# Triangular inverses of a gated delta rule: 32x32 diagonal blocks on tiles of the array instead of whole 128x128 matrices

## The chip, the core and the metric

One core of a Trainium2 chip runs the whole program. The metric is the device time of one execution in microseconds (us), taken as the median of several runs. A difference of about 0.3% is what a measurement of this kernel can tell from no change.

The core's engines are PE (TensorE, with its weight loads shown apart as PEld), DVE (VectorE), ACT (ScalarE), POOL (GpSimd) and SP (which here issues DMAs). They run side by side and wait for each other on semaphores.

## What is computed

Two layers of a decoder trunk on 512 tokens of width 1024. Each layer has four token mixers, a merge of their outputs through gates, and a gated feed-forward part. The change is inside one of the mixers, the gated delta rule (4 heads, chunks of 64 tokens), of which this is the part that matters:

```python
decay = where(tril, exp(G[..., :, None] - G[..., None, :]), 0)
L = where(strict, einsum('bnhid,bnhjd->bnhij', k * beta, k) * decay, 0)
T = triangular_solve(eye + L, eye, lower=True, unit_diagonal=True)   # the inverse
u = einsum('bnhij,bnhjd->bnhid', T, v * beta)
w = einsum('bnhij,bnhjd->bnhid', T, k * beta * exp(G))
# then a recurrence over the chunks with u, w and a state
```

The kernel takes chunks of 128 tokens, so there are 4 chunks x 4 heads = 16 lower triangular matrices of 128x128 a layer, and each is inverted.

## The kernel before

**Weights.** All weights stream from memory in slabs of 512 KB: SP loads a slab to `raw` (2 buffers), ACT rounds it to a high part `wH` (L1061), POOL or DVE makes the low part `wL` (L2034, L1422), and PE multiplies with three products for each pair of tiles (L489 to L491). 3 slabs can be split ahead.

**Fillers.** A layer's projections that nobody needs at once are kept as fillers. `fill(n)` on PE does n of them (`column_tile`, 24 matmuls of 128x512 each), and the table `FILL` says how many stand at which place of the mixers. The same `fill` on ACT moves the result out of its bank (L1064), splits the next slab (L1061) and stores the result. The order on every engine is that in which the code is written; each engine works through its own list.

**The inverse.** The 16 matrices (units) stand transposed or not in four buffers of the tile `arena`: `mL` holds L, `mU` the inverse as it grows (transposed, upper triangular), `mT` the transpose of `mU`, `mY` a product. They are handled in four batches of 4 units, one PSUM bank a batch. The method doubles the size of the blocks whose inverse is known: 1, 2, 4, ... 64 to 128, seven levels.

- Level 0: PE transposes L (L697), DVE masks it to pairs (L1717) and subtracts it from the identity (L1719).
- Levels 1 to 6, for each of the four batches: PE forms `mL`·`mU` (`y_product`, L708) and transposes `mU` (`t_transpose`, L718); DVE masks the product (L1723) to the blocks of this level (`lev`); ACT copies the transpose out (L1233); PE multiplies the two (`u_product`, L728); DVE subtracts the result from `mU` (L1729). Every product is of full 128x128 matrices whatever the level, since the mask picks the blocks.
- The batches are staggered by hand so that PE has another batch to work on while DVE and ACT serve one.

A float32 matmul is recorded as two instructions on PE and two weight loads (two passes); a transpose as one. So `L708 x8` is four products.

**Around it.** Ahead of the inverse PE forms k·k and q·k (L688), then does two fillers (`FILL["skq"]`), while POOL makes `qd` (L2081) and DVE multiplies q·k by the decay (L1705, `at_part`). One filler stands after the fifth of the six levels (`FILL["level"]`). After the inverse PE forms w (L753), and the recurrence over the four chunks begins (L762 and on).

Of the kernel before, what the change touches and what calls it, by code (L numbers as in the profile page):

```python
# [23 lines left out]
P = 128  # L24
# [45 lines left out]
        "turn": 0, "skq": 2, "level": [0, 0, 0, 0, 1, 0], "chunk": [1, 1, 1, 0], "oss": 1,  # L70
# [19 lines left out]
def _slabs():  # L90
# [8 lines left out]
    for dt in range(KT):  # L99
# [12 lines left out]
             "du_ps": 24, "fg_tanh": 22, "ga_ready": 44, "gate_tanh": 8, "gdn_done": 2, "gexp_ready": 1,  # L112
# [11 lines left out]
             "ss_ps": 2, "st_ready": 17, "su_ps": 4, "t_cos": 3, "t_ps": 24, "t_ready": 24, "t_sin": 4,  # L124
             "tanh_ready": 6, "tr_ps": 4, "tr_taken": 4, "trig_done": 6, "u0_ready": 8, "u_chunks": 4,
             "u_ready": 24, "vn_ps": 4, "vn_ready": 4, "vt_ps": 1, "vt_ready": 1, "wexp_ready": 16, "wt_ps": 4,
             "wt_ready": 4, "x_ready": 2, "xo_ready": 8, "y0_ps": 4, "y5_ps": 2, "y5_ready": 2, "y5_sq": 2,
             "y5_tanh": 4, "y_ps": 24, "y_ready": 24, "z_copied": 16, "z_tanh": 2}
# [21 lines left out]
def _const_columns():  # L150
    at = 0
    for name, n in [("ones", P), ("ident", P), ("blk", P), ("le", P), ("ge", P), ("lt", P),
                    ("gt", P), ("lev", 7 * P), ("rot", P), ("freq", 1), ("stack", 32), ("cneg", NT * NCMP),
                    ("c01", NT * NCMP), ("t", P)]:
        CK[name] = (at, n)
        at += n
    return at
# [34 lines left out]
def program(nc, a_x, a_pos, a_const, a_pack, a_w, a_gates, a_out):  # L192
    with ExitStack() as ctx:
# [64 lines left out]
        lev = cst("lev").rearrange("p (l c) -> p l c", l=7)  # L258
# [20 lines left out]
            skk_ps l_part skq_ps at_part y0_ps u0_ready  # L279
            y_ps y_ready du_ps u_ready t_ps t_ready wt_ps wt_ready  # L280
# [37 lines left out]
        mL, mU, mT, mY = mats  # L318
        cv = arena[:, 8192:11264].rearrange("p (t s) -> p t s", t=6)
# [108 lines left out]
        with nc.Block() as block:  # L428
# [30 lines left out]
            def _(pe):  # L459
                for layer in range(DEPTH):  # L460
# [230 lines left out]
                    fill(FILL["skq"])  # L691

                    pe.wait_ge(*of("bt_taken", 6))
                    for b in range(4):
                        pe.wait_ge(*of("at_part", b + 1))
                        for j in range(4):
                            last = nc.tensor.transpose(PS[2 + b][:, P * j:P * j + P], mL[:, 4 * b + j, :], ident)  # L697
                        last.then_inc(q["y0_ps"], 1)
                    def y_product(n):
                        b = n % 4  # L700
                        if n >= 4:
                            pe.wait_ge(*of("u_ready", n - 3))
                        else:
                            pe.wait_ge(*of("u0_ready", 2 * n + 2))
                        if n >= 2:
                            pe.wait_ge(*of("y_ready", n - 1))
                        for j in range(4):
                            last = mm(PS[2 + n % 2][:, P * j:P * j + P], mL[:, 4 * b + j, :], mU[:, 4 * b + j, :],  # L708
                                      start=True, stop=True)
                        last.then_inc(q["y_ps"], 1)  # L710

                    def t_transpose(n):

                        b = n % 4
                        if n >= 2:
                            pe.wait_ge(*of("t_ready", n - 1))
                        for j in range(4):
                            last = nc.tensor.transpose(PS[6 + n % 2][:, P * j:P * j + P], mU[:, 4 * b + j, :], ident)  # L718
                        last.then_inc(q["t_ps"], 1)

                    def u_product(n):
                        b = n % 4
                        pe.wait_ge(*of("y_ready", n + 1))
                        pe.wait_ge(*of("t_ready", n + 1))
                        if n >= 2:
                            pe.wait_ge(*of("u_ready", n - 1))
                        for j in range(4):
                            last = mm(PS[4 + n % 2][:, P * j:P * j + P], mT[:, 4 * b + j, :], mY[:, 4 * b + j, :],  # L728
                                      start=True, stop=True)
                        last.then_inc(q["du_ps"], 1)  # L730

                    pe.wait_ge(*of("kc_ready", 1))
                    for lv in range(6):
                        n = 4 * lv
                        y_product(n)
                        t_transpose(n)
                        y_product(n + 1)
                        t_transpose(n + 1)
                        u_product(n)
                        y_product(n + 2)  # L740
                        t_transpose(n + 2)
                        u_product(n + 1)
                        y_product(n + 3)
                        t_transpose(n + 3)
                        u_product(n + 2)
                        u_product(n + 3)
                        fill(FILL["level"][lv])

                    pe.wait_ge(*of("u_ready", 24))
# [277 lines left out]
            def _(a):  # L1027
                act = nc.scalar.activation
                chain, split = [0], [0]
                for layer in range(DEPTH):  # L1030
# [200 lines left out]
                    for n in range(24):  # L1231
                        a.wait_ge(*of("t_ps", n + 1))
                        act(mT_flat[:, S * (n % 4):S * (n % 4) + S], PS[6 + n % 2][:, :], ACT.Copy).then_inc(q["t_ready"], 1)  # L1233
                        if n % 4 == 3:
                            fill(FILL["level"][n // 4])
# [166 lines left out]
            def _(v):  # L1402
                chain = [0]
                for layer in range(DEPTH):
# [295 lines left out]

                    v.wait_ge(*of("skq_ps", 4))
                    v.wait_ge(*of("qd_ready", 8))
# [5 lines left out]
                    def four(x):  # L1708
                        return x.unsqueeze(1).broadcast_to([P, 4, P])

                    def bank4(b):
                        return PS[b][:, :].rearrange("p (u c) -> p u c", u=4)

                    for b in range(4):
                        u = slice(4 * b, 4 * b + 4)
                        v.wait_ge(*of("y0_ps", b + 1))
                        tt_(mY[:, u, :], bank4(2 + b), four(lev[:, 0, :]), M).then_inc(q["u0_ready"], 1)  # L1717
                        v.wait_ge(*of("u0_ready", 2 * b + 1))
                        tt_(mU[:, u, :], four(ident), mY[:, u, :], SU).then_inc(q["u0_ready"], 1)  # L1719
                    def y_mask(n):  # L1720
                        b = n % 4
                        v.wait_ge(*of("y_ps", n + 1))
                        tt_(mY[:, 4 * b:4 * b + 4, :], bank4(2 + n % 2), four(lev[:, 1 + n // 4, :]), M)\  # L1723
                            .then_inc(q["y_ready"], 1)

                    def u_update(n):
                        u = slice(4 * (n % 4), 4 * (n % 4) + 4)
# [540 lines left out]
```

## Time and profile before

| | us |
|---|---|
| median of 3 runs | 2095.03 (2090.07 to 2096.05) |
| the profiled execution | 2093.96 |
| its span, first to last instruction | 2092.1 |
| PE busy | 2003.3 |
| DVE busy | 1120.0 |
| ACT busy | 779.3 |
| POOL busy | 421.1 |
| last product of q·k to the first product for w, layer 1 | 191.49 to 268.32 |

The profiled execution is 1.9 us longer than its span and 1.1 us under the median. Times in the trace are counted from the start of the span. Matmuls overlap, so PE's busy time is a union of intervals.

### The profile page before, as it was taken

To read this page: it belongs to the slowest core of one execution; us is meant where nothing else is said; L and a number is where in the kernel's file an instruction comes from. 1 tells how busy PE (TensorE), PEld (TensorE's weight loads), DVE (VectorE), ACT (ScalarE), POOL (GpSimd) and SP (SyncE) were. 2 spreads that over 40 slices of the span, in tenths; PEclk is the share of its full clock that TensorE was granted. 3 is DMA by queue.
4 is the path that set the end of the run, shared out by engine and by line. 5 is a ranking of instruction groups with operands and counts; after the bars stand their busy time and mean duration, and the time that the engine had idled before them with its cause. 6 is when DMAs were issued, how large, how long until landed. Compare 5 with 4: busy or idle time off the path is not lost.

```text
span 2092.1 us, 25542 instructions
## 1 busy us (share of the span) xinstructions
PE 2003.3 (96%) x9988; PEld 1607.9 (77%) x9988; DVE 1120.0 (54%) x1702; ACT 779.3 (37%) x1182; POOL 421.1 (20%) x240
## 2 busy tenths in 40 slices
PE   7999989899999999999999999999999999999999
PEld 5677978567677888888876789776677778888887
DVE  6955547553466555543369265565523765555422
ACT  5542253553344332222244422526532543232221
POOL 2436012223153000000035350122321610000000
PEclk9999999999999999999999989999999999999999
DMA  5332012212153333333343210112121633333332
GB/s 199 115 117 62 11 56 81 76 51 76 56 216 107 101 100 96 96 101 101 111 161 96 89 53 16 61 66 81 58 74 59 228 101 91 93 98 101 101 101 101
DMA packets 57133, 196.45 MB, mean 94 GB/s; under 512 B 6464, under 2 KB 6976, under 8 KB 54848
## 3 DMA queue, kind: packets, MB, share of 16 engines
q1 hardware_dynamic: 42912, 152.49, 23.2%
q10 hardware_dynamic: 14112, 42.41, 5.3%
q8 instruction: 79, 1.29, 0.3%
q14 instruction: 30, 0.25, 0.0%
HBM read 176.01 MB, written 18.87 MB: 93 GB/s over the span
## 4 chain that ended last, share of the span: by engine, by line
PE 86%; DVE 9%; ACT 2%; POOL 1%; issue 1%; DMA 1%; SPq 0%; ACTq 0%; DVEq 0%; PEldq 0%; POOLq 0%
PE bank L489 22%; PE bank L491 22%; PE bank L490 22%; PE bank L728 2%; PE bank L708 2%; PE bank L958 2%; PE bank L846 2%; PE bank L919 1%; PE bank L827 1%; PE bank L718 1%; DVE arena L1804 1%; PE bank L855 1%; PE bank L627 1%; DVE arena L1465 1%; PE bank L836 1%
## 5 line engine op out<-in xcount | busy, mean ns | idle before, releaser
L489 PE MATMUL bank<-hH,wH 128*128 128x512 f32 (+1 forms) x1536 | 616.7, 402 | 22.2 <-DVE hL L1431 10.2
L490 PE MATMUL bank<-hL,wH 128*128 128x512 f32 (+1 forms) x1536 | 604.3, 393 | 0.0
L491 PE MATMUL bank<-hH,wL 128*128 128x512 f32 (+1 forms) x1536 | 604.2, 393 | 0.0
L2034 POOL TENSOR_TENSOR wL<-raw,wH 128x1024 fp32r<-128x1024 f32 (+1 forms) x114 | 274.5, 2411 | 1188.0 <-ACT wH L1061 1187.8
L1061 ACT ACTIVATE wH<-raw 128x1024 fp32r<-128x1024 f32 (+1 forms) x276 | 288.1, 1046 | 255.9 <-PE bank L491 215.6
L489 PEld LDWEIGHTS bank<-hH,wH 128*128 128x128 f32 (+1 forms) x1536 | 291.0, 189 | 99.9 <-issue 25.1
L491 PEld LDWEIGHTS bank<-hH,wL 128*128 128x128 f32 (+1 forms) x1536 | 290.4, 189 | 64.7 <-issue 0.8
L490 PEld LDWEIGHTS bank<-hL,wH 128*128 128x128 f32 (+1 forms) x1536 | 291.0, 189 | 61.9 <-issue 2.6
L1422 DVE TENSOR_TENSOR wL<-raw,wH 128x1024 fp32r<-128x1024 f32 x162 | 214.1, 1321 | 212.5 <-ACT wH L1061 211.8
L1064 ACT ACTIVATE gst<-bank 128x512 f32<-128x512 f32 x64 | 38.2, 597 | 275.4 <-PE bank L491 275.4
L491 PE MATMUL bank<-hidH,wL 128*128 128x512 f32 x352 | 140.4, 399 | 0.0
L490 PE MATMUL bank<-hidL,wH 128*128 128x512 f32 x352 | 138.7, 394 | 0.0
L489 PE MATMUL bank<-hidH,wH 128*128 128x512 f32 x352 | 138.0, 392 | 0.0
L1384 ACT ACTIVATE hidH<-arena 128x512 fp32r<-128x512 f32 x44 | 27.9, 633 | 191.3 <-DVE arena L2002 191.3
L1920 DVE TENSOR_REDUCE small<-bank 128x1 f32<-128x128 f32 (+3 forms) x64 | 30.8, 489 | 114.4 <-PE bank L921 113.0
L2104 POOL TENSOR_TENSOR arena<-arena 128x512 f32<-128x512 f32 x48 | 79.2, 1651 | 25.4 <-DVE arena L1962 21.4
L490 PEld LDWEIGHTS bank<-hidL,wH 128*128 128x128 f32 x352 | 66.1, 188 | 17.0
L489 PEld LDWEIGHTS bank<-hidH,wH 128*128 128x128 f32 x352 | 66.1, 188 | 15.9
L491 PEld LDWEIGHTS bank<-hidH,wL 128*128 128x128 f32 x352 | 66.1, 188 | 15.3
L1381 ACT ACTIVATE comp<-comp 128x512 f32<-128x512 f32 x44 | 27.8, 632 | 127.6 <-DVE comp L1993 127.6
L1233 ACT ACTIVATE arena<-bank 128x512 f32<-128x512 f32 x48 | 28.6, 597 | 78.8 <-PE bank L718 78.8
L1993 DVE TENSOR_TENSOR comp<-bank,vt 128x512 f32<-128x512 f32 x44 | 30.4, 691 | 48.4 <-PE bank L491 43.0
(398 smaller groups left out, 2835.6 us busy)
## 6 DMA issues: line engine op xcount, KB each, us to landing
raw<-weights SPq DMA_DIRECT2D x279, 512.0 KB, 3.5
gates<-gst ACTq DMA_DIRECT2D x64, 256.0 KB, 2.4
gload<-gates ACTq DMA_DIRECT2D x16, 1024.0 KB, 7.2
arena<-weights ACTq DMA_DIRECT2D x10, 512.0 KB, 5.4
xT<-x SPq DMA_DIRECT2D x4, 512.0 KB, 6.3
pj<-weights ACTq DMA_DIRECT2D x4, 512.0 KB, 4.0
out<-xT SPq DMA_DIRECT2D x8, 256.0 KB, 4.2
const<-constants SPq DMA_DIRECT2D x1, 1100.5 KB, 6.6
```

The costliest lines, as they stand in the source:

```text
L489: mm(out, a[0], b[0], start=start, stop=False)
L490: mm(out, a[0], b[1], start=False, stop=False)
L491: return mm(out, a[1], b[0], start=False, stop=stop)
L708: last = mm(PS[2 + n % 2][:, P * j:P * j + P], mL[:, 4 * b + j, :], mU[:, 4 * b + j, :], start=True, stop=True)
L728: last = mm(PS[4 + n % 2][:, P * j:P * j + P], mT[:, 4 * b + j, :], mY[:, 4 * b + j, :], start=True, stop=True)
L846: last = mm(out[:, P * (j - kb):S - P * kb], cst("ge") if j == kb else ones, sb_sp(h, j)[:, P * j:S], start=(j == kb), stop=(j == NT - 1), ...
L958: last = mm(PS[6 + br][:, HD * h:HD * h + HD], npt[:, kb, P * h:P * h + P], nvt[:, kb, HD * br:HD * br + HD], start=(kb == 0), stop=(kb == ...
L1061: act(h, x, ACT.Copy).then_inc(q["w_high"], 1)
L1064: act(out, stream(name)[:, :], ACT.Copy, scale=scale).then_inc(q["proj_taken"], 1)
L1422: tt_(wL[:, ORD[i] % SPLIT], raw[:, i % RING], wH[:, ORD[i] % SPLIT].bitcast(F32), SU)\
L2034: tt_(l, x, h.bitcast(F32), SU).then_inc(slab_taken[i % RING], 1)
L2104: ins = tt_(mtmp[:, dt % 2, 0, :], mtmp[:, dt % 2, 0, :], mtmp[:, dt % 2, m, :], A_)
```

## The change

The inverse is built in two parts.

- **Diagonal blocks of 32.** Each 128x128 matrix has four diagonal blocks of 32x32. Blocks, not whole matrices, go through levels 0 to 4 (block sizes 1 to 32). A matmul takes rows 32b to 32b+32 of its operands and writes the same rows of a bank: one 32x32 tile of the array for each b. Both the inverse (`uc32`) and its transpose (`ut32`) are carried, each updated by its own product, so there is no transpose. The 16 units are in two halves of 8, which share nothing; PE's two products for a level are `block_y` (32 matmuls a half) and `block_u` (64 a half, 32 at level 0).
- **Levels 32 and 64 as blocks.** The blocks are copied into `mU` (zeroed by POOL ahead of time) and `ut64`. Then the off-diagonal blocks of 32 (80 matmuls of 32x32) and of 64 (32 matmuls of 64x64) are formed with products of just those blocks; copies go half to ACT, half to DVE.
- **Order.** `block_y` of level 0 stands ahead of the two fillers; DVE's first masks stand ahead of its multiplications by the decay (L1705). The filler inside the inverse stays after the fifth level (n = 4), which is now the last of the small ones. ACT's 24 copies (L1233) are gone; ACT has 6 copies after level 4, ahead of its part of that filler, and 5 in the block levels.
- The table of masks shrinks from 7x128 to 5x32 columns, with an identity of 32 columns.

The core of the diff:

```diff
+                    def block_y(n, g):
+                        out = PS[(2, 7)[g]]
+                        for u in UNIT_HALF[g]:
+                            for b in range(4):
+                                last = mm(out[rows(b), 32 * (u % 8):32 * (u % 8) + 32], mL[rows(b), u, rows(b)],
+                                          uc32[rows(b), u, :] if n else cst("id32")[rows(b), :], start=True, stop=True)
+                        last.then_inc(q["y_ps"], 1)
+                    def block_u(n, g):
+                        for u in UNIT_HALF[g]:
+                            c = slice(32 * (u % 8), 32 * (u % 8) + 32)
+                            if n:
+                                for b in range(4):
+                                    mm(PS[3 + g][rows(b), c], ut32[rows(b), u, :], y32[rows(b), u, :], start=True, stop=True)
+                            for b in range(4):
+                                last = mm(PS[5 + g][rows(b), c], y32[rows(b), u, :],
+                                          ut32[rows(b), u, :] if n else cst("id32")[rows(b), :], start=True, stop=True)
+                        last.then_inc(q["du_ps"], 1)
+                    pe.wait_ge(*of("bt_taken", 6))
+                    for g in range(2):
+                        block_y(0, g)
                     fill(FILL["skq"])
-                    for lv in range(6):
-                        y_product(n) ... t_transpose(n) ... u_product(n)
+                    pe.wait_ge(*of("at_part", 4))
+                    for n in range(5):
+                        for g in range(2):
+                            if n:
+                                pe.wait_ge(*of("u_ready", 2 * n + g - 1))
+                                block_y(n, g)
+                        for g in range(2):
+                            pe.wait_ge(*of("y_ready", 2 * n + g + 1))
+                            block_u(n, g)
+                        fill(FILL["level"][n])
+                    pe.wait_ge(*of("u_ready", 10))
...
+                    for g in range(2):
+                        for u in UNIT_HALF[g]:
+                            last = mm(PS[5 + g][0:64, HD * (u % 8):HD * (u % 8) + HD], mL[64:128, u, 0:64], mU[64:128, u, 64:128],
+                                      start=True, stop=True)
+                        last.then_inc(q["y_ps"], 1)
...
+                    for g in range(2):
+                        pe.wait_ge(*of(("y_copied", "y_ready")[g], (2, 12)[g]))
+                        for u in UNIT_HALF[g]:
+                            last = mm(PS[(7, 2)[g]][0:64, HD * (u % 8):HD * (u % 8) + HD], ut64[:, u, :], y64[:, u, :],
+                                      start=True, stop=True)
+                        last.then_inc(q["du_ps"], 1)
```

On PE, before, one level for two of its four batches stands like this (first level; L708 products with `mU`, L718 transposes, L728 the second product):

```order
L708 MATMUL bank<-arena 128x128 [waits u0_ready,kc_ready]
L708 MATMUL bank<-arena 128x128 x3
L718 MATMUL bank<-const,arena 128x128 x4
L708 MATMUL bank<-arena 128x128 [waits u0_ready]
L708 MATMUL bank<-arena 128x128 x3
L718 MATMUL bank<-const,arena 128x128 x4
L728 MATMUL bank<-arena 128x128 [waits t_ready,y_ready]
L728 MATMUL bank<-arena 128x128 x3
```

On PE in the changed kernel, the same place, from the start of level 1 (L703 is `block_y`, L712 and L714 the two products of `block_u`):

```order
L703 MATMUL bank<-arena 32x32 [waits u_ready]
L703 MATMUL bank<-arena 32x32 x31
L703 MATMUL bank<-arena 32x32 [waits u_ready]
L703 MATMUL bank<-arena 32x32 x31
L712 MATMUL bank<-arena 32x32 [waits y_ready]
L712 MATMUL bank<-arena 32x32 x3
L714 MATMUL bank<-arena 32x32 x4
L712 MATMUL bank<-arena 32x32 x4
```

A level was 48 instructions of 128x128 (16 + 16 transposes + 16) and is now 192 of 32x32 (64 + 64 + 64), with four waits instead of one for each batch and step.

On DVE, between the multiplication of k·k by the decay and level 1, before:

```order
L1699 TENSOR_TENSOR arena<-bank,arena 128x512 [waits dmask_ready,skk_ps] x4
L1705 TENSOR_TENSOR arena<-bank,arena 128x512 [waits qd_ready,skq_ps]
L1705 TENSOR_TENSOR arena<-bank,arena 128x512 x3
L1717 TENSOR_TENSOR arena<-bank,const 128x512 [waits y0_ps]
L1719 TENSOR_TENSOR arena<-const,arena 128x512 [waits u0_ready]
```

and after (L1734 and L1759 are the old L1699 and L1705; L1749 masks, L1771 and L1772 update the inverse and its transpose, L1774 starts the transpose):

```order
L1734 TENSOR_TENSOR arena<-bank,arena 128x512 [waits dmask_ready,skk_ps] x4
L1749 TENSOR_TENSOR arena<-bank,const 128x256 [waits y_ps,qd_ready]
L1749 TENSOR_TENSOR arena<-bank,const 128x256 [waits y_ps]
L1755 TENSOR_TENSOR arena<-const,arena 128x256 [waits y_ready] x2
L1759 TENSOR_TENSOR arena<-bank,arena 128x512 [waits skq_ps]
L1759 TENSOR_TENSOR arena<-bank,arena 128x512 x3
L1763 MEMSET arena 32x16x32 [waits at_part]
L1774 TENSOR_TENSOR arena<-const,bank 128x256 [waits du_ps] x2
L1749 TENSOR_TENSOR arena<-bank,const 128x256 [waits y_ps] x2
L1771 TENSOR_TENSOR arena<-arena,bank 128x256 [waits du_ps]
L1772 TENSOR_TENSOR arena<-arena,bank 128x256
```

Four instructions of 128x256 came ahead of the multiplications by the decay, and a level is 6 instructions of 128x256 instead of 8 of 128x512.

On PE, from the end of the filler inside the inverse to w, the changed kernel has (L737, L744 and L745 the blocks of 32, L751 and L758 those of 64, L767 is w); before, the sixth full level and then w stood here:

```order
L737 MATMUL bank<-arena 32x32 [waits u_ready]
L737 MATMUL bank<-arena 32x32 x31
L744 MATMUL bank<-arena 32x32 [waits y_ready,y_copied]
...
L751 MATMUL bank<-arena 64x64 [waits u_ready,u_copied]
L751 MATMUL bank<-arena 64x64 x15
L758 MATMUL bank<-arena 64x64 [waits y_copied,u_copied]
L758 MATMUL bank<-arena 64x64 x7
L758 MATMUL bank<-arena 64x64 [waits y_ready]
L758 MATMUL bank<-arena 64x64 x7
L767 MATMUL bank<-arena,pj 64x128 [waits u_ready,u_copied]
```

The last level became a chain of five steps, each of which waits for copies by ACT and DVE.

## Rows read from the trace of the kernel before

**Rows 1.** The page's part 1 (busy time) and part 4 (share of the last chain).

```profile
PE 2003.3 (96%) x9988; PEld 1607.9 (77%) x9988; DVE 1120.0 (54%) x1702; ACT 779.3 (37%) x1182; POOL 421.1 (20%) x240
...
PE 86%; DVE 9%; ACT 2%; POOL 1%; issue 1%; DMA 1%; SPq 0%; ACTq 0%; DVEq 0%; PEldq 0%; POOLq 0%
```

**Rows 2.** The chain, 170 to 320: start us, us, engine, tile, line.

```profile
190.40 1.16 PE bank L688 x8
...
226.17 0.89 PE bank L708 x8
227.06 0.44 PE bank L718 x4
...
235.14 0.89 PE bank L708 x8
...
268.32 1.99 PE bank L753 x32
```

**Rows 3.** Windows: busy us of each engine (instructions), granted clock, DMA share.

```profile
191.49:202.30 10.81, 10.81 (x49) 8.95 (x49) 2.48 (x4) 1.54 (x2) 8.61 (x10) 1.00 0.25 76
202.30:268.30 66.00, 62.19 (x522) 60.23 (x520) 39.64 (x57) 17.31 (x28) 4.74 (x2) 1.00 0.11 33
252.80:258.40 5.60, 5.60 (x27) 4.63 (x26) 0.72 (x2) 0.00 (x0) 0.00 (x0) 1.00 0.00 0
...
1239.00:1305.00 66.00, 62.17 (x523) 60.27 (x523) 39.75 (x57) 17.31 (x28) 4.74 (x2) 1.00 0.11 33
```

**Rows 4.** Windows of L600 (69.30), then of L627 (161.30): PE, PEld, clock.

```profile
69.30:69.35 0.05, 0.03 (x4) 0.03 (x5) 1.00 0.00 0
...
161.30:161.37 0.07, 0.03 (x4) 0.03 (x5) 1.00 0.00 0
```

**Rows 5.** Sequencer of PE, waits in three windows: ns min/median/max, first to last start.

```profile
L706 PEldq EVENT_SEMAPHORE  x2: 51/51/51, 216.1 to 216.4; - x2
...
L726 PEldq EVENT_SEMAPHORE  x1: 1480/1480/1480, 217.7 to 217.7; - x1
...
L706 PEldq EVENT_SEMAPHORE  x1: 51/51/51, 219.3 to 219.3; - x1
```

**Rows 6.** Timeline: start, us, engine, line, shapes; idle before it and its releaser.

```profile
161.34 7.16 PE L627 MATMUL bank<-vt,pj 128*32 128x128 f32 x128
...
198.49 2.48 DVE L1705 TENSOR_TENSOR arena<-bank,arena 128x512 f32<-128x512 f32 x4 [8.14 <-POOL arena L2081]
...
199.01 2.40 POOL L2034 TENSOR_TENSOR wL<-raw,wH 128x1024 fp32r<-128x1024 f32 x1 [0.62 <-ACT wH L1061]
...
227.53 0.60 ACT L1233 ACTIVATE arena<-bank 128x512 f32<-128x512 f32 x1 [2.60 <-PE bank L718]
228.43 0.69 DVE L1723 TENSOR_TENSOR arena<-bank,const 128x512 f32<-128x512 f32 x1 [0.64 <-PE bank L708]
...
258.67 0.60 ACT L1064 ACTIVATE gst<-bank 128x512 f32<-128x512 f32 x1 [6.82 <-PE bank L491]
259.16 1.05 ACT L1061 ACTIVATE wH<-raw 128x1024 fp32r<-128x1024 f32 x1
...
270.77 1.10 PE L762 MATMUL bank<-pj,arena 128*128 128x64 f32 x8 [0.48 <-ACT arena L1238]
```

**Rows 7.** Groups by line and shape, window 268 to 303 and the first layer.

```profile
L1745 DVE COPY arena<-bank 128x256 f32<-128x256 f32 x4 | 1.7, 425 | 12.6 <-PE bank L770 12.6
...
L627 PE MATMUL bank<-vt,pj 128*32 128x32 f32 x32 | 4.4, 229 | 0.0
```

**Rows 8.** Windows of PE alone: busy us (instructions), granted clock.

```profile
466.20:469.48 3.28, 3.28 (x33) 1.00 0.00 0
469.48:473.00 3.52, 3.52 (x10) 0.52 0.00 0
473.00:476.00 3.00, 3.00 (x15) 0.99 0.00 0
...
1217.20:1230.80 13.60, 13.60 (x66) 0.50 0.12 39
```

More of the change, by code:

```diff
@@ L69 @@
 FILL = {"blocks": [1, 1, 1, 1, 1, 1, 1, 1], "hidden": 1, "gelu": 1, "gsum": 2, "qk": 1, "grow": 1,
[L70 removed]
+        "turn": 0, "skq": 2, "level": [0, 0, 0, 0, 1], "chunk": [1, 1, 1, 0], "oss": 1,
         "s5": [3, 2], "glu": 2, "sb": [2, 1, 1, 1, 1], "norms": 1, "rot": 2,
@@ L690, in _ @@
                             last.then_inc(q[done], 1)
-                    fill(FILL["skq"])
[L693 to L708, printed above, removed]
+                    UNIT_HALF = [range(0, 8), range(8, 16)]
@@ new lines, in _ @@
+                    pe.wait_ge(*of("u_ready", 10))
+                    for u in range(16):
+                        for b in (0, 2):
+                            last = mm(PS[2][rows(b), 32 * u:32 * u + 32], mL[rows(b + 1), u, rows(b)], uc32[rows(b + 1), u, :],
+                                      start=True, stop=True)
+                    last.then_inc(q["y_ps"], 1)
+                    pe.wait_ge(*of("y_copied", 1))
+                    pe.wait_ge(*of("y_ready", 11))
+                    for u in range(16):
+                        for b in (0, 2):
+                            mm(PS[3][rows(b), 32 * u:32 * u + 32], ut32[rows(b), u, :], y32[rows(b), u, :], start=True, stop=True)
+                        last = mm(PS[4][rows(1), 32 * u:32 * u + 32], y32[rows(0), u, :], ut32[rows(0), u, :], start=True, stop=True)
@@ L721, in u_product @@
[L721 to L728, printed above, removed]
+                    pe.wait_ge(*of("u_copied", 2))
@@ new lines, in _ @@
+                    for n in range(5):
+                        if n:
+                            for g in range(2):
+                                y_mask(n, g)
+                        for g in range(2):
+                            v.wait_ge(*of("du_ps", 2 * n + g + 1))
+                            if n:
+                                tt_(half_of(uc32, g), half_of(uc32, g), half_bank(3 + g), SU)
+                                tt_(half_of(ut32, g), half_of(ut32, g), half_bank(5 + g), SU).then_inc(q["u_ready"], 1)
+                            else:
+                                tt_(half_of(ut32, g), eight(cst("id32")), half_bank(5 + g), SU).then_inc(q["u_ready"], 1)
@@ L2222, in _constants @@
     put("gt", r > c)
-    lev = np.zeros((P, 7, P))
-    for n in range(7):
+    lev = np.zeros((P, 5, 32))
+    a, b = r % 32, np.arange(32)[None, :]
+    for n in range(5):
         s = 1 << n
-        lev[:, n] = (r // (2 * s) == c // (2 * s)) & (r % (2 * s) < s) & (c % (2 * s) >= s)
+        lev[:, n] = (a // (2 * s) == b // (2 * s)) & (a % (2 * s) < s) & (b % (2 * s) >= s)
     put("lev", lev)
+    put("id32", a == b)
     rot = np.zeros((P, P))
```

141 lines of the change are left out of this document (74 added, 67 removed).

## The prediction

> **What bounds the kernel now.** I read the busy shares first, then the last chain, then that chain inside the inverse, then the windows around it. PE is busy 96% of the span and the chain runs through PE for 86% [rows 1], so PE's own time counts nearly everywhere. In the inverse, one level of six takes 235.14 - 226.17 = 8.97 us [rows 2]. Its 80 PE instructions (16 products of two passes, 16 transposes of one, 16 products of two) go at 0.89 us for 8, which is 0.111 each or 8.9 us a level: PE is full. DVE's and ACT's pieces are done inside that time [rows 6]. The windows say the same for both layers: PE is busy 62.2 of 66.0 us from 202.3 and from 1239, DVE 39.6, ACT 17.3, at full clock [rows 3]. So the stage is worth what PE issues in it. I count it from the end of the last q·k products (191.49) to the first product for w (268.32): 76.8 us a layer [rows 2], 10.8 for two fillers and 5.6 for the third [rows 3], and 60.4 for the inverse.
>
> **What the change takes off.** All 60.4 us of that: the transposes of level 0, six full levels, and the waits at both ends. ACT loses 24 copies, DVE 56 operations of 128x512; neither was late, so this alone is worth nothing.
>
> **What it puts there.** Per layer 976 matmuls of 32x32 (64 and 64 at level 0, 4 x 192, 32 and 48 at level 32) and 32 of 64x64. Before there were 304 of 128x128. What one of the 32x32 costs decides everything; the trace has none, so I bound it.
>
> - *From below: the tiles.* The products of 32-column weights write four column tiles in turn, and four of them start within 0.07 us (0.05 for L600) [rows 4]: tiles side by side run together. A pass over 128 columns takes 0.111 us, so one over 32 columns takes about 0.028 (estimate), a product of two passes 0.056, and four at once 14 ns each.
> - *The feed.* PE's sequencer must hand out each product. Two of its waits, with eight matmuls between them, stand 0.3 us apart, 0.05 of it the wait itself: about 31 ns each. After a wait that ends at 217.7 + 1.48 = 219.2, four products are out by 219.3: about 25 ns each [rows 5].
> - *From above.* If tiles took turns, 56 ns. 128 passes of L627 take 7.16 us [rows 6], 112 ns a product, but those have up to 128 columns.
>
> I take 25 ns, the feed, since it lies above the 14 ns of the tiles and a level will keep the feed going without a pause; 14 and 56 stay as ends. A product of 64x64 on one tile: two passes over 64 columns, 2 x 0.055 = 0.11 us; the upper end is 0.22, from the 8 passes over 64 columns in 1.10 us of L762, whose weights are twice as wide [rows 6].
>
> The Trainium skill, TensorE: Matmul & The Clock Gate (Part 1), states that start-to-start never drops below about 25 ns however small N is. Taken for each pass, that would be 50 ns a product, and the case of a slow feed below. Here the trace disagrees at least for a handful of passes: four starts in 0.05 us [rows 4].
>
> **The other engines in a level.** DVE has six operations of 128x256; the nearest row, a copy of that size from PSUM, takes 0.425 us [rows 7], back to back about 0.35 (a 128x512 repeats every 0.62: 2.48 for four [rows 6]). From the last matmul's start to the next engine I allow 0.27 (a 32-column pass is recorded with 0.229 [rows 7]), and 0.06 back. The two halves alternate: while DVE masks one half (0.27 + 0.42 + 0.06 = 0.75) PE does the other's 32 products (0.8 us at 25 ns), so PE does not wait there. After `block_u` DVE needs 0.27 + 0.35 + 0.42 + 0.06 = 1.1 us for a half, PE is busy 0.8 with the other half's `block_y`: 0.3 us of wait a level, three times. A level is then 192 x 0.025 + 0.3 = 5.1 us. If the products took 14 ns, the loop of DVE and PE would set a level at 3.3.
>
> **The block levels.** After the filler ACT must first empty its bank and split a slab (0.60 + 1.05 [rows 6]), so its copy of the first product ends about 2.5 us after the filler where PE needed 0.8: 1.8 us of wait. Then a DVE copy ahead of the products of 64 (0.27 + 0.6 + 0.06 = 0.9; 0.60 is ACT's copy of 128x512 and these hold as many columns [rows 6]), nothing between the two products of 64 since their halves cover each other, and 0.9 before w: 3.7 with the small pieces.
>
> **Moved and added steps, costed at nothing.** `block_y` of level 0 is now ahead of the fillers; its time is counted, and it delays them by 1.6 us. DVE's four new operations (1.7 us) delay the decay multiplications, which ran from 198.49 to 200.97 [rows 6]: they end about 202.7, and PE, with two fillers and 1.6 us, comes at 203.9. That is 1.2 us of cover; without it, PE waits. POOL's clearing of 128x2048 stands ahead of its next low part, which began at 199.01; a 128x1024 operation takes 2.4 us, so at most 4.8 us [rows 6], and the next filler is 20 us away. ACT waits for the clearing, long done. SP's queue changes nowhere but in 360 KB less of constants at the start, early enough to be worth zero.
>
> **The sum at full clock.** 976 x 0.025 = 24.4, 32 x 0.11 = 3.5, fillers 10.8 + 5.5 = 16.3, waits 0.9 + 3.7 = 4.6: 48.8 us in place of 76.8, a gain of 28.0 a layer.
>
> **The clock.** After 3.3 us of PE with products of 31 columns (L889, 33 instructions) the granted clock was 0.52 for the next 3.5 us, with PE busy all the time: 10 filler matmuls there, against 15 in the next 3.0 [rows 8]. In layer 2 it was 0.50 for 13.6 us from 1217.2 on, after a stretch of short bursts. These are the levels of 1.2 and 2.4 GHz. The new stage is 25 us of products of 32 columns, the nearest thing in the trace is L889, so I take the lower level through it. It costs 32 x 0.104 = 3.3 us at the products of 64, 1.7 at the filler (half of 3.4), 1.9 at w (1.99 us [rows 2] at twice the time), and 1.2 in the levels (the tiles now need 28 ns, 3 over the feed, for about half of the 768). Together 8.1; the gain is 19.9 a layer, 39.8 in all.
>
> 2093.96 - 39.8 = 2054.2 for the profiled execution; the median of the runs lies 1.1 above that: **2055 us**.
>
> **Rivals.**
>
> 1. *The clock holds.* All four tiles busy may look like a busy array, as it does through L627 (clock 1.00 in its window [rows 4]). Gain 28.0 a layer: 2039. For it: PE never pauses. Against: L889, also without a pause.
> 2. *The tiles set the pace.* The feed is faster than I read it (rows with one decimal) and a level is the loop of 3.3 to 4.0 us, at 14 to 18 ns: gain 33.6 to 36.7 a layer, 2022 to 2028.
> 3. *The feed is slower.* 976 products are 4000 instructions in 25 us; nothing in the trace asks for such a rate for longer than a few. At 31 to 40 ns (first reading of rows 5, and half as much again) each ns costs 0.98 us a layer and the 0.9 us of waits in the levels go: with the lower clock's 6.9 the gain is 16.1 at 31 and 7.4 at 40, 2063 to 2080; at 50 ns it would be 2100.
> 4. *The tiles take turns* (slower). The four tiles of a product group write the same bank at the same columns from different rows of the array. L600 and L627 use all 128 rows, so no row shows this. If a bank takes one row group at a time, a product costs its own 56 ns: a level is 192 x 0.056 = 10.75 us where it was 8.97 and the stage 77.3 at full clock: 2096. At the lower clock the 56 become 112, and the stage is 62 us longer than now: 2219. If each also waits for the last one's write, 0.229 [rows 7], the kernel is over 2400. It decides from about 48 ns a product (22.0 us of gain left without the 0.9 of waits, over 0.976 us for each ns).
>
> The Trainium skill, TensorEngine Tiling (Array Packing), Gotcha 1, states that different row tiles cannot access the same PSUM bank simultaneously. By that rule it would be rival 4. No run here shows it; the case for the forecast is only that different partitions of the bank are written.
>
> **How the numbers follow.** Forecast 2055: 0.34. Clock holds: 0.25. Tiles set the pace: 0.11. Slower feed: 0.16, nearly all faster than now. Turns: 0.12. Something else that eats the gain, near no change: 0.02. A measurement of this kernel can tell 0.3%, that is 6 us, from no change. Faster by more than that: 0.34 + 0.25 + 0.11 + 0.14 = 0.84. Within: 0.04. Slower: 0.12. The range takes in the forecast, both quick cases and the slower feed up to 40 ns, and leaves out the turns and the ends: 2022 to 2088.
>
> **What the profile would show.** A level of `block_y` and `block_u`: 5 us if the feed sets it, 3.3 if the loop does, 10.75 if tiles take turns, with starts of the four tiles 7 ns or 28 ns and more apart. The granted clock from 210 on: 0.5 (forecast) or 1.0. DVE idle before L1771 for PE, and PE not idle before L712. After the filler, PE idle until ACT's copy L1262. The stage 48.8 us (clock holds) or about 55, with w 1.9 longer. I am wrong if a level takes over 8 us, if the decay multiplications (L1759) end after PE has come, or if the next stages give the time back: the chunks and the S5 part wait for DVE and ACT, which have more slack now, not less.

## The result, and the profile after

The changed kernel takes **2103.75 us** (median of six runs, 2098.14 to 2109.39), the kernel before, run beside it, 2094.87 (2090.07 to 2096.05): a ratio of 1.0045, with a 95% interval from 1.0031 to 1.0059. It is slower by about 9 us or 0.45%, where the forecast was 2055 and the range 2022 to 2088. The profiled executions span 2104.3 and 2092.1 us.

The page of the changed kernel, parts 1, 3 and 4 (they answer to [rows 1]; the first line is busy us, share and instructions of each engine):

```profile
PE 1972.1 (94%) x13028; PEld 1572.7 (75%) x13028; DVE 1065.5 (51%) x1660; ACT 763.9 (36%) x1156; POOL 426.1 (20%) x242
...
q8 instruction: 103, 1.69, 0.3%
...
PE 82%; DVE 10%; issue 4%; ACT 2%; POOL 2%; DMA 1%; POOLq 0%; SPq 0%; ACTq 0%; DVEq 0%; PEldq 0%
```

PE is busy for 31 us less than before, as meant. But "issue", time in which the engine waits for nothing that the profile shows, went from 1% to 4% of the chain, and PE has 3040 matmuls and 3040 weight loads more. That is 6080 instructions more, and the queue that carries the instructions moved 103 packets of 16 KB where the kernel before moved 79:

```profile
q8 instruction: 79, 1.29, 0.3%
```

24 packets for 6080 instructions fits 256 instructions of 64 bytes in each. Where the issue time lies is told by the chain through levels 1 and 2 and the start of level 3 of the first layer (start us, us, what; the longest pieces), which stands where [rows 2] had one product after the other:

```profile
204.14 1.04 PE bank L703 x85
205.18 2.46 issue
207.64 0.41 PE bank L703 x26
208.95 3.51 issue
212.46 0.26 PE bank L712 x2
214.40 2.07 issue
216.46 0.26 PE bank L712 x2
217.10 1.60 PE bank L703 x98
218.70 1.49 issue
220.19 0.58 PE bank L703 x26
222.12 1.80 issue
223.92 0.26 PE bank L712 x2
225.85 1.53 issue
227.38 0.26 PE bank L712 x2
228.01 1.60 PE bank L703 x98
229.62 1.21 issue
```

Two things are to be seen. In a burst the products are quicker than forecast. The chain holds only 85 of the 100 passes of the first burst of level 1, so the rate is read from the timeline; the granted clock there is 1.00:

```profile
204.10 1.08 PE L703 MATMUL bank<-arena 32*32 32x32 f32 x100
```

Without the last pass's own 0.19 us, 100 passes start within 0.89 us: 9 ns each, 18 a product. At a clock of 0.50 it is 13 a pass and 26 a product, from the first `block_y` of the second layer (1.86 us less 0.24):

```profile
1230.93 1.86 PE bank L703 x128
```

And no burst lasts: PE works 1.3 to 2.3 us and stands still for 1.2 to 3.5, three times a level. PE's waits over the whole span put a sum to this (us in total, times, longest):

```profile
PE bank L712 <- issue: 30.5, 16, 3.5
PE bank L703 <- issue: 13.9, 8, 2.5
```

These are 24 stalls, three in each of four levels of both layers, and 44.4 us or 22.2 a layer. The groups by line from the end of one stall to the end of the next, 230.8 to 234.2 (columns as in part 5 of a page: line, engine, operation, tiles, count, busy us, mean ns, idle time before), count what is in a burst:

```profile
L712 PE MATMUL bank<-arena 32*32 32x32 f32 x52 | 1.6, 236 | 0.0
L712 PEld LDWEIGHTS bank<-arena 32*32 32x32 f32 x52 | 1.5, 152 | 0.0
L714 PE MATMUL bank<-arena 32*32 32x32 f32 x48 | 1.5, 236 | 0.0
L714 PEld LDWEIGHTS bank<-arena 32*32 32x32 f32 x48 | 1.4, 152 | 0.0
L703 PE MATMUL bank<-arena 32*32 32x32 f32 x28 | 0.6, 239 | 1.2 <-issue 1.2
L703 PEld LDWEIGHTS bank<-arena 32*32 32x32 f32 x28 | 0.5, 148 | 1.3 <-issue 1.3
```

128 matmuls and 128 loads: 256 instructions, one packet, whatever lines they come from. The other bursts between two stalls of levels 1 to 3 hold 128 and 128 as well. The DMA view of the changed kernel over the same levels, 217 to 249 us, in slices of 0.8 us (GB/s), shows the packets one by one:

```profile
GB/s 0 20 0 0 0 20 0 0 0 20 0 0 0 0 20 0 0 0 20 0 0 0 0 20 0 0 0 20 0 0 0 20 0 0 0 20 0 0 0 0
...
q8 instruction: 9, 0.15, 1.8%
```

Nine packets, four to five slices apart: 27.2 us for eight steps, 3.4 each, and three fetches are a level. In the same window the kernel before needs three:

```profile
q8 instruction: 3, 0.05, 0.8%
```

The levels themselves, in windows from the first `block_y` (L703) of levels 2, 3 and 4 to that of the next, or to the filler (window, length, then busy us and instructions of each engine, granted clock, DMA share):

```profile
217.10:228.01 10.91, 6.09 (x403) 5.56 (x396) 2.35 (x6) 0.00 (x0) 0.00 (x0) 0.50 0.02 5
228.01:238.38 10.37, 6.11 (x403) 5.58 (x396) 2.35 (x6) 0.00 (x0) 0.00 (x0) 0.50 0.02 5
238.38:249.01 10.63, 6.09 (x383) 5.49 (x373) 2.35 (x6) 0.00 (x0) 0.00 (x0) 0.50 0.02 5
```

A level takes 10.4 to 10.9 us, where one took 8.97 before and 5.1 was forecast. Level 1, whose fetches run beside the slabs of weights, takes 12.96 (204.14 to 217.10). From the end of the q·k products (190.55) to w (268.66) are 78.1 us, against 76.8. Most of the rest of the loss lies behind: the chunk stage from w to the output's L795 (now L809), before and after,

```profile
268.32:305.34 37.02, 32.25 (x217) 28.12 (x217) 19.38 (x31) 19.12 (x32) 7.08 (x3) 1.00 0.18 56
```

```profile
268.66:309.13 40.47, 35.76 (x217) 31.68 (x217) 19.30 (x30) 19.09 (x32) 7.09 (x3) 0.88 0.16 52
```

has the same instructions and takes 3.4 us longer, at a granted clock of 0.88 in place of 1.00. Half of this, 1.7 us, is w itself at its start.

### The profile page after: what moved, and what is told of

Read it like the earlier page. It is cut to its first block, busy times and chain, and to the rows that moved or that the text cites. A ratio compares the mean times of both kernels' runs of the same rounds, so it can differ in the third digit from the quotient of the medians.

```text
span 2104.3 us, 31472 instructions
## 1 busy us (share of the span) xinstructions
PE 1972.1 (94%) x13028; PEld 1572.7 (75%) x13028; DVE 1065.5 (51%) x1660; ACT 763.9 (36%) x1156; POOL 426.1 (20%) x242
## 4 chain that ended last, share of the span: by engine, by line
PE 82%; DVE 10%; issue 4%; ACT 2%; POOL 2%; DMA 1%; POOLq 0%; SPq 0%; ACTq 0%; DVEq 0%; PEldq 0%
PE bank L491 21%; PE bank L493 21%; PE bank L492 21%; PE bank L860 2%; PE bank L972 2%; PE bank L933 1%; DVE wL L1457 1%; DVE arena L2010 1%; DVE arena L1852 1%; PE bank L703 1%; PE bank L869 1%; PE bank L841 1%; PE bank L712 1%; PE bank L714 1%; PE bank L629 1%
## 5 line engine op out<-in xcount | busy, mean ns | idle before, releaser
L1457 DVE TENSOR_TENSOR wL<-raw,wH 128x1024 fp32r<-128x1024 f32 x162 | 214.1, 1322 | 212.9 <-ACT wH L1075 212.2
L492 PEld LDWEIGHTS bank<-hidL,wH 128*128 128x128 f32 x352 | 66.1, 188 | 17.1
L712 PE MATMUL bank<-arena 32*32 32x32 f32 x1024 | 31.8, 234 | 30.5 <-issue 30.5
```

Source lines behind the costliest of these rows:

```text
L492: mm(out, a[0], b[1], start=False, stop=False)
L712: mm(PS[3 + g][rows(b), c], ut32[rows(b), u, :], y32[rows(b), u, :], start=True, stop=True)
L1457: tt_(wL[:, ORD[i] % SPLIT], raw[:, i % RING], wH[:, ORD[i] % SPLIT].bitcast(F32), SU)\
```

## The experiments

**Theory A, the instruction fetch.** PE can hold one block of 256 instructions beyond the one that it works on, and a block arrives about 3.5 us after the last one was begun. A product of 32x32 in float32 is four instructions (two passes, each a load and a matmul), so 64 products are a block, and no matter how fast the array is, they cost 3.5 us: 55 ns a product. The rivals: the array is slow (tiles take turns, or the lower clock), or the loop between TensorE and VectorE sets the level.

**wide: twice the columns, the same instructions.** Every product of levels 1 to 4 streams 64 columns.

```
-  uc32[rows(b), u, :]
+  uc32[rows(b), u - u % 2:u - u % 2 + 2, :]      # and likewise y32, ut32; 64 columns of out
```

> Each 32x32 product of levels 1 to 4 streams 64 columns instead of 32 (its own and its neighbour's), so the values are not the reference's; the instructions, waits and tiles stay the same in number. Theory A (the instruction fetch: the engine gets its instructions in blocks of 16 KB, and one block, 64 products, arrives every 3.5 us): a level, read from the first L703 of one level to that of the next, stays at 10.4 to 10.9 us and the whole kernel within 5 us of 2104. Theory B (the array: tiles take turns, or the lower clock makes a pass slow): a product costs by its columns, and a level goes from 10.4 to 15 us or more, the kernel to 2140 or more.

2099.80 us in one run. The windows of levels 2 to 4:

```profile
218.04:228.52 10.48, 7.58 (x398) 7.01 (x392) 2.35 (x6) 0.00 (x0) 0.00 (x0) 0.83 0.02 5
228.52:238.89 10.37, 6.22 (x400) 5.62 (x392) 2.35 (x6) 0.00 (x0) 0.00 (x0) 1.00 0.02 5
238.89:249.25 10.36, 6.21 (x383) 5.51 (x371) 2.35 (x6) 0.00 (x0) 0.00 (x0) 1.00 0.02 5
```

Twice the work on the array costs nothing, and neither does the clock change the level: at 1.00 a level takes what it took at 0.50. The array isn't what sets it. What the clock does cost shows right behind, in the filler after level 4: 5.67 us at a clock of 1.00 here, 7.8 at 0.73 in the changed kernel.

**third: a third of the products left out.** The products for U (L712) in levels 1 to 4 are gone.

```
-  for b in range(4):
-      mm(PS[3 + g][rows(b), c], ut32[rows(b), u, :], y32[rows(b), u, :], start=True, stop=True)
```

> Leaves out the 64 products a level that update U (L712) in levels 1 to 4; VectorE's operations stay as many, the update of U reads the other bank. Theory A (fetch): 512 instructions a level are two blocks instead of three, so 7.0 us a level instead of 10.4, and 4 x 3.5 x 2 layers = 28 us off the kernel: about 2076. Rival (the waits between TensorE and VectorE set the level): a level stays above 9.5 us and the kernel above 2095.

2073.51 us; the levels took 7.18, 7.73 and 6.91 us with the same six VectorE operations in each. Two blocks in place of three, as theory A has it; a loop with VectorE would have stayed.

**halves: the same products in half the instructions.** In levels 1 to 4 the operands are read as their upper 16 bits, so a product is one pass.

```
+  def upper(x):
+      return x.bitcast(BF16).rearrange("p (c two) -> p c two", two=2)[:, :, 1]
-  mm(..., ut32[rows(b), u, :], y32[rows(b), u, :], ...)
+  mm(..., upper(ut32[rows(b), u, :]), upper(y32[rows(b), u, :]), ...)
```

> The 768 products a layer of levels 1 to 4 take the upper 16 bits of their float32 operands (as bfloat16), so the values are coarser than the reference's; the products, their tiles, columns, waits and VectorE's operations are the same, but each product is one pass, two instructions instead of four. Theory A (fetch, 3.5 us for 256 instructions): 384 instructions a level, 1.5 blocks, 5.2 us in place of 10.4, which is 4 x 5.2 x 2 = 41 us off the kernel: 2062, within 2054 to 2070. Rival (the loop of TensorE and VectorE, or the array's clock, sets a level once the products are cheap): a level of 7 us or more, 2077 or more.

2065.14 us in one run, and w starts at 247.4 instead of 268.66: 21.3 us less in the first layer, 5.3 a level. Between two stalls (212.9 to 216.65) stand again 128 matmuls, which are now 128 products:

```profile
L715 PE MATMUL bank<-arena 32*32 32x32 bf16 x52 | 1.2, 190 | 0.0
L717 PE MATMUL bank<-arena 32*32 32x32 bf16 x48 | 1.1, 187 | 0.0
...
L706 PE MATMUL bank<-arena 32*32 32x32 bf16 x28 | 0.4, 186 | 1.9 <-issue 1.9
```

The products, the tiles and the waits are those of the changed kernel; only the passes are half as many, and with them the instructions, and the level is half as long. That fewer passes mean less work for the array too is no other explanation, since in wide twice the work cost nothing. This is the run that shows the cause most directly.

**hybrid: only the last two levels as blocks.** The kernel before, with its levels 0 to 4 on the whole array, the transpose of U taken once, then the block levels of 32 and 64 (32 + 48 + 32 products).

```
-  for lv in range(6):
+  for lv in range(4):
       ...
+  t_transpose(16 + b) for b in range(4); Y by 32 products of 32x32; fill(1)
+  48 products of 32x32, then 16 + 16 of 64x64, off mU and mT
```

> The kernel before, with levels 0 to 4 as they were on the whole array, and only the last two levels as blocks (32 products of 32x32 for Y, 48 for the updates, 32 of 64x64), the transpose of U taken once by 16 transposes. Few instructions (about 450 in the block part), so theory A expects no stall by fetch: two levels of 8.97 us go, 1.8 for transposes, 0.8, 1.2 and 3.4 for products and 1.8 of waits come: 9 us less a layer, 2077, within 2070 to 2085. If small products are slow in themselves (56 ns or more each, and the 64x64 at the lower clock), it is 2085 to 2095.

2091.77 us, a ratio of 0.9983 (0.9971 to 0.9995): faster by its interval, but by 4 us, less than the 0.3% that a measurement of this kernel can tell, and not by 18. The chain at the end of the stage says why (start us, us, what):

```profile
245.85 1.13 PE bank L759 x64
...
257.47 3.45 PE bank L781 x32
...
261.77 3.70 PE bank L790 x32
265.92 1.97 PE bank L799 x8
```

64 passes of 32x32 in 1.13 us and w at 261.77, 6.6 us earlier than in [rows 2]: no stall worth naming, as theory A expects of so few instructions. But w takes 3.70 us where it took 1.99 [rows 2], and the first products of the chunks 1.97 where they took 1.10 [rows 6], at the lower level of the clock; the whole chunk stage takes 40.7 us, near the 40.5 of the changed kernel, not 37.02. In the second layer it takes 37.0 (1300.1 to 1337.1), and this execution is the fastest of ten, 2086.98. So the miss is in part the clock behind the blocks, and in part the way from the filler to the products of 64x64, 2.7 us (252.70 to 255.40) with PE idle for 1.6 of them, where 1.8 was allowed for all waits of the block part; what the median of 2091.77 lost beyond this no trace shows.

**spread: three fillers behind levels 1, 2 and 3.**

```
-  "skq": 2, "level": [0, 0, 0, 0, 1], "chunk": [1, 1, 1, 0]
+  "skq": 1, "level": [0, 1, 1, 1, 1], "chunk": [0, 0, 1, 0]
```

> Only the places of three fillers a layer are changed: one of the two ahead of level 0, and two of the chunk stage, are issued behind levels 1, 2 and 3. Theory A (fetch): a filler of 5.4 us has 48 instructions, and while it runs the fetch gets one and a half to two blocks ahead, so each moved filler saves 3 to 4 us of the stalls: 18 to 24 us less than 2104, of which the uncovered waits in the chunk stage and ahead of level 0 may take back 5 to 10: 2085 to 2095. Theory B (the array or the clock makes the products slow): a filler costs its own time wherever it stands, and the time is 2104 or more with the waits uncovered in the chunks.

2119.80 us, 1.0100 of before (1.0067 to 1.0133): slower than the changed kernel, and my reading of how far the fetch runs ahead was wrong. Filler, level 2, filler, level 3:

```profile
215.47:222.93 7.46, 7.46 (x32) 5.77 (x34) 0.75 (x2) 0.00 (x0) 0.00 (x0) 0.75 0.01 2
222.93:233.38 10.45, 4.21 (x386) 3.85 (x385) 1.60 (x4) 1.54 (x2) 2.34 (x1) 0.81 0.23 78
233.38:240.40 7.02, 7.02 (x28) 5.46 (x32) 0.75 (x2) 0.00 (x0) 0.00 (x0) 0.79 0.01 2
240.40:250.49 10.09, 4.31 (x386) 3.98 (x385) 1.60 (x4) 1.54 (x2) 2.34 (x1) 0.81 0.26 81
```

A filler is only 48 instructions, but 7 us in which the fetch could run. It doesn't: a level behind it takes 10.1 to 10.5 us all the same, with two stalls in place of three that are longer (2.18 and 4.06 us from 225.19 on). The queue of instructions moved one packet during the first filler (215.4 to 223) and two during the level behind it. That is one block ahead and not two. The later blocks come slower where slabs are loaded beside them (78 GB/s in the window, 5 in the changed kernel's levels 2 to 4); that the slabs are the reason was not tested. The chunk stage also missed its two fillers: 36.5 us in place of 40.5, so 4.0 saved of some 11, with 4.7 us of waits for VectorE that were none before.

**weave: the same fillers, inside the levels.** If only one block is held ahead, a block costs the longer of 3.5 us and its own work, and long work must stand inside each block.

```
+  def weave(products):          # called after every 4 or 8 products of a level
+      count[0] += products
+      if count[0] >= 24:        # then three matmuls 128x512 of the level's filler
+          count[0] -= 24
+          next(steps[0], None)
```

> The same fillers in the same levels as in spread, but the filler of levels 1, 2 and 3 is woven in: after every 24 products of 32x32 three filler matmuls of 512 columns are issued. Theory A, as the trace of spread has sharpened it (the engine holds one block of 256 instructions beyond the one it executes, asks for the next when it starts one, and gets it 3.5 us later, so each block costs the longer of 3.5 us and its own work): a level with its filler is 816 instructions, 3.2 blocks, 11.2 to 12 us, where it was 17.5 in spread; about 6 us for each of six levels, 36 us less than the 2120 of spread, 2084, within 2072 to 2095. Rival (the fillers slow the fetch, since their weights come by the same DMA engines, or the array is what is full): 17 us a level again and 2115 or more.

2095.99 us, 1.0015 of before (1.0001 to 1.0028): 24 us less than spread with the same work in the same levels, where I had expected 36; just outside the range.

> As weave, but the chunk stage keeps its three fillers and the two that the levels need more are taken from the S5 part ([3, 2] becomes [2, 1]). Theory A: the levels are as in weave; spread lost 6.9 us a layer in the chunks by their fillers' going, and if the S5 part has work enough without its two, this is 10 us or so less than weave: 2071, within 2062 to 2085. If the S5 part's waits take the place of the fillers, it is no better than weave.

weave_s5 leaves the chunks their fillers and takes two from the S5 part. **2085.65 us**, 0.9966 (0.9953 to 0.9979): faster than both kernels by itself, though not 2071. Two of its woven levels, each with a whole filler in it:

```profile
215.46:227.25 11.79, 11.70 (x413) 7.95 (x413) 2.35 (x6) 1.54 (x2) 2.38 (x1) 1.00 0.21 71
227.25:239.78 12.53, 11.72 (x413) 8.03 (x416) 2.35 (x6) 1.54 (x2) 2.38 (x1) 1.00 0.20 67
```

11.8 to 12.5 us for level and filler, 17.1 to 17.9 in spread, and PE is busy in nearly all of it. So a woven filler adds 1 to 2 us to a level, where one behind it adds 5.4 to 7.8. What was missing of the 2071: one of the three had stood ahead of level 0, where PE now waits 2.3 us for the decay multiplications, and level 4, which isn't woven, still stalls twice.

**weave_late and weave_more: which fillers can be had?**

> As weave_s5, but both fillers ahead of level 0 stay (so that TensorE has work while VectorE ends the decay multiplications), the S5 part keeps all of its five, and the three more that the levels take come from behind it: one from the GLU, one from the first softplus-attention head, one ahead of the NSA scores. Theory A: the fetch hides the three, and the stage is about as long as in the changed kernel plus the one unwoven thing, so 3 x 5.4 us a layer less 2 to 4 of uncovered waits behind: 2104 - 24 to 28 = 2076 to 2080. If the later stages need their fillers as the S5 part did, it comes out at 2085 to 2092.

2101.02 us, 1.0027 (1.0011 to 1.0043). The stage, with three more fillers in it, takes 82.6 us in the first layer, as expected, and 87.6 in the second, where the changed kernel took 78 and 79. More is lost behind: the three fillers taken from the GLU, the attention and the rotations had been cover. PE's waits for others over the whole span:

```profile
PE bank L868 <- DVE arena L1879: 14.1, 2, 7.1
...
PE bank L960 <- DVE arena L1971: 11.4, 2, 5.7
...
PE bank L877 <- ACT arena L1348: 8.5, 4, 4.1
```

In the changed kernel the first stood at 6.9 (its L841 for L1852), the third at 2.5 (L850), and the second was none.

> As weave_late, with one filler more taken from the S5 part and woven into level 4, whose filler behind it stays. Level 4 takes 10.4 us in weave_s5, 6.1 of it stalls by the fetch, so theory A says that this filler too costs nothing there: 5 us a layer less where nothing waits for it, 2068; if the S5 part misses it, as it did in weave_s5, the gain is 0 to 3 a layer, 2074 to 2080.

2095.36 us, 1.0004 (0.9990 to 1.0018): one more, woven into level 4, comes with 6 us less. But the wait of L960 fell from 11.4 to 6.5 between the two traces, so how much of this is the weaving stays open; the waits of L868 and L877 stay. Both runs took longer than even the case against them allowed.

**weave_l4 and weave_skq: two trims of weave_s5.**

> weave_s5 with the filler of level 4 woven into that level as well, so that none stands behind it. Theory A: level 4 and its filler took 10.4 + 7.4 us in weave_s5 and take 11.5 now; the wait for ScalarE's slab and split copies, which the filler hid, costs 2.5 more. About 3 us less a layer, and the S5 part's chain on VectorE comes earlier with it, so it counts in full: 2080, within 2074 to 2085.

2084.60 us, 0.9951 (0.9935 to 0.9968).

> weave_s5 with the second filler ahead of level 0 back in its place and none behind level 4. TensorE was idle for about 5 us ahead of level 0 in weave_s5, waiting for the decay multiplications, so that filler costs nothing there; the one behind level 4 took 5.4 to 7.4 and hid 2.5 of waits: 3 to 5 us less a layer, 2078, within 2072 to 2085. If the wait ahead of level 0 is a longer chain that only starts with the fillers (POOL and ScalarE come later), it is the same as weave_s5, 2086.

2088.11 us, 0.9966 (0.9956 to 0.9976). Neither can be told from weave_s5. For weave_skq the expectation had 5 us of idle time ahead of level 0, where weave_s5 had 2.3; that wait is gone, and PE's for ScalarE behind level 4 grew from 2.3 us to 4.6 over the two layers. In weave_l4 the filler is hidden, but the wait that it had covered is 4.8 us and not 2.5:

```profile
PE bank L771 <- ACT arena L1289: 4.8, 1, 4.8
```

**halves_l4: the same trim on halves.**

> halves (upper 16 bits of the operands in levels 1 to 4, one pass a product), with the stage's own last filler woven into level 4 in place of behind it; no filler comes from another stage. Theory A: level 4 with its filler is 432 instructions, 1.7 blocks, 6 us, where it took 5.2 + 7.4; the wait for ScalarE's copies that the filler hid costs 2.5. About 4 us less a layer than halves: 2057, within 2050 to 2064. If TensorE and VectorE already set the pace of a halved level, the weaving gives nothing and it is 2065 or more.

2069.40 us, 0.9874 (0.9857 to 0.9890). It is no faster than halves' one run, so no gain by the trim can be seen. The stage of the first layer is 3.5 us longer than in halves, and here too the wait behind level 4 has grown, from 1.2 us:

```profile
PE bank L774 <- ACT arena L1292: 4.9, 1, 4.9
```

ScalarE does its split copies and the filler's own copies there, one after the other, and only then the copy that PE needs.

Faster than both kernels are so, in float32, weave_l4, weave_s5 and weave_skq by 0.3 to 0.5% of before, and with 16-bit operands in four levels halves_l4 by 1.3%, which is coarser arithmetic and not the same trade.

## Why the prediction was wrong, step by step

**What bounds the kernel: right, and not enough.** PE was full, and taking work off it was worth time. But the kernel's PE has two speeds that matter, that of the array and that of its supply with instructions, and the second had no row of its own in the trace of before: at 160 instructions in 8.97 us a block of 256 lasts 14 us.

**A product at 25 ns: too slow for a burst.** It takes 18 ns there at full clock, in the range of rival 2, and 26 at the lower level, where I had put 28. So neither the tiles nor the handing out of products cost more than forecast, and the eight matmuls of [rows 5] did not show the feed at its limit.

**"A level will keep the feed going without a pause": this is the step that failed.** The feed was read from eight matmuls between two waits [rows 5] and carried over to 976 products. Rival 3 named the doubt, that 4000 instructions in 25 us were never asked for, and then priced it with the same handful of rows at 31 to 40 ns, with a chance of 0.16. It came out at 10.6 us / 192 = 55 ns over a level. The four levels cost 44.9 us (204.14 to 249.01) where the sum had 4 x 5.1 = 20.4: 24.5 us a layer, more than the 19.9 of forecast gain. 22.2 of them are the stalls, a term that the sum did not have.

**Rival 4, tiles that take turns: its numbers came, its mechanism didn't.** It gave 10.75 us a level and 56 ns a product, and a level takes 10.4 to 10.9. Its 77.3 us for the stage takes the 0.9 us of waits off twice; by its own terms it is 78.2, or 2098, and the stage took 78.1. Who looks only at these lengths finds it confirmed, by coincidence. Inside the level it is refuted: in a burst, products on four row tiles of one bank pass at 18 ns where 56 was the estimate for a tile alone, and with twice the columns (wide) a level is as long. The Trainium skill, TensorEngine Tiling (Array Packing), Gotcha 1, says that different row tiles cannot access the same bank at once; here passes on four of them overlap in one bank, in different partitions, and the measurement decides. The rule of the Trainium skill, TensorE: Matmul & The Clock Gate (Part 1), of at least 25 ns from start to start doesn't hold for these tiles either, whose passes start 9 ns apart.

**The loop of TensorE and VectorE: never in play.** The 0.3 us of wait a level can't be seen beside stalls of 1.2 to 1.8. In halves it appears, as nine waits of PE for L1775 of up to 0.6 us, 3.6 in all.

**The clock: right in place and size, short in reach.** The granted clock was 0.50 in the levels, and the 64x64 products took 3.32 and 3.06 us (forecast 3.5 + 3.3 for both), w 3.70 (1.99 + 1.9), the filler 7.8 (5.5 + 1.7). What I left out is that it stays low into the chunk stage: of the 3.4 us that this stage lost, 1.7 are w, which the sum had, and 1.7 lie behind it.

**Steps costed at nothing: right.** PE's waits in the trace hold none for the decay multiplications, with both fillers ahead, and ScalarE's none for the clearing. "DVE and ACT have more slack now" was right too, and gave nothing.

**The stage in sum.** Forecast 55 to 57, measured 78.1, before 76.8: +1.3 in the first layer; in the second, from the end of the q·k products to w, 79.3 us (1230.94 to 1310.21) against 79.2. The chunks lose 3.4 and 3.3. Together this is 8.1 of the 12.2 us between the two spans. The other 4 are the net of all other stages. A part is again the clock: from L850 (before L836) to the fillers behind L860 (L846) both layers take 26.0 us at a granted clock of 0.87, where they took 23.7 and 23.6 at 1.00, and on the way there, from L820 on, 62.8 and 62.6 in place of 64.2 and 64.3, at 0.97 in place of 0.95. Why the low stretches of the clock fall elsewhere, so far behind the blocks, and what the rest is, no run here shows.

The Trainium skill, Runtime: NRT & Kernel Launch, section Instruction fetch mechanics, has the mechanism: blocks of 16 KiB with 256 instructions, fetched one block ahead while the last is executed. The runs agree with this, in the packets, in the stall after every 256th instruction and in the failure of spread. It goes on that the fetch is hidden since the sequencer dispatches more slowly than the memory fills; here it isn't. It also gives TensorE a store of 2048 instructions; after a filler of 7 us the levels of spread ran for less than two blocks until they stood.

## What to carry to other kernels

Count a stage's instructions as well as its matmul time: here PE got 256 instructions in 3.4 us at best, so a stage of many blocks cost at least 13.3 ns for each load and each matmul, and cutting full products into tiles multiplies just these (from 160 to 768 for a level here). A rate read from a burst of eight must not be carried over to thousands; look in the trace for the longest stretch at the rate that the new code needs, and where there is none, let the range include the slow case with more than a small chance. Where many short instructions can't be avoided, put the long ones between them and not behind them, and take only fillers that cover nothing where they stand.

## What the runs showed of the hardware

- PE's instructions come in packets of 16 KB, 256 to a packet. In levels 2 to 4 one came every 3.4 us (nine packets), and PE stood for 1.2 to 1.8 us after every 256th instruction. Beside slabs of weights (78 to 86 GB/s in those windows) the longest stalls were 3.5 to 4.1 us.
- Only one packet is held ahead: 7 us of long matmuls didn't shorten the next level (10.45 us against 10.4 to 10.9).
- Four 32x32 tiles on the diagonal, writing one bank, run side by side: their passes start 9 ns apart at full clock, 13 at the lower level, and each is recorded with about 0.2 us.
- The granted clock was 0.50 in levels 2 to 4 with 32 columns a pass, 0.83, 1.00 and 1.00 with 64 columns and the same instructions, and 1.00 in levels 2 and 3 of weave_s5, with PE busy for 23.4 of 24.3 us there.
